# A two-layer encoder trunk in float32 on one NeuronCore: Strassen's algorithm for most of the gated layers' first product

## The reference

```python
D_MODEL, BATCH, SEQ, DEPTH = 1024, 1, 512, 2
FFN_DIM = ((8 * D_MODEL // 3 + 127) // 128) * 128            # 2816

def _conv_glu_ffn(x, w_in, conv_w, conv_b, w_down):
    gate, up = jnp.split(x @ w_in, 2, axis=-1)
    gate = lax.conv_general_dilated(gate, conv_w[:, None, :], window_strides=(1,),
        padding=[(1, 1)], dimension_numbers=('NWC', 'WIO', 'NWC'),
        feature_group_count=FFN_DIM) + conv_b
    return (jax.nn.gelu(gate, approximate=False) * up) @ w_down

def reference(x, ...):
    for i in range(DEPTH):
        if i % 2 == 0: h = _chunked_spatial_gating(x, ...)
        else:          h = _diff_attention(x, positions, ...)
        x = _layer_norm(DEEPNORM_ALPHA * x + h, ln_g[i, 0], ln_b[i, 0])
        h = _conv_glu_ffn(x, f_w_in[i], f_conv_w[i], f_conv_b[i], f_w_down[i])
        x = _layer_norm(DEEPNORM_ALPHA * x + h, ln_g[i, 1], ln_b[i, 1])
    return x
```

## Time and profile before

| | |
|---|---|
| median of three runs | 1276.57 us (1276.24 to 1276.88) |
| the profiled execution, its own time | 1277.31 us |
| its span, first to last instruction | 1275.6 us |
| PE busy | 1266.0 us, 99% |
| DVE, ACT, POOL busy | 650.2, 459.4, 165.1 us |
| mean granted clock of PE | 0.999 of full |

### The profile page before, as it was taken

One profiled execution on the slowest core, in us unless ns is written; L12 is line 12 of the kernel. 1 busy time (PEld: TensorE's weight loads), 2 busy tenths in 40 slices (PEclk: granted clock), 3 DMA queues, 4 the chain that ended last, 5 costly groups with the idle time before them and its releaser, 6 DMA issues.

```text
span 1275.6 us, 15660 instructions
## 1 busy us (share of the span) xinstructions
PE 1266.0 (99%) x6096; PEld 1055.6 (83%) x6096; DVE 650.2 (51%) x890; ACT 459.4 (36%) x553; POOL 165.1 (13%) x159
## 2 busy tenths in 40 slices
PE   9999999999999999999999999999999999999997
PEld 7888888889888888888888877788988888888886
DVE  3637877346343434433372777775743334343346
ACT  3422333322232323322314588775143222232230
POOL 3001100040000000000224444453100000000001
PEclk9999999999999999999999999999999999999999
DMA  8434564250433232222522334235032333232221
GB/s 269 146 96 124 173 176 147 89 185 2 131 99 99 87 99 80 98 97 99 188 74 71 100 105 124 91 108 166 33 99 99 99 99 99 99 99 100 96 102 66
DMA packets 104652, 140.64 MB, mean 110 GB/s; under 512 B 9440, under 2 KB 81464, under 8 KB 104352
## 3 DMA queue, kind: packets, MB, share of 16 engines
q1 hardware_dynamic: 95024, 127.81, 31.2%
q0 software_dynamic: 9440, 12.11, 2.9%
q10 hardware_dynamic: 144, 0.13, 0.0%
HBM read 137.85 MB, written 10.52 MB: 116 GB/s over the span
## 4 chain that ended last, share of the span: by engine, by line
PE 98%; DVE 1%; DMA 0%; ACT 0%; issue 0%; POOL 0%; DVEq 0%; SPq 0%; POOLq 0%
PE bank L1263 31%; PE bank L1267 31%; PE bank L1266 31%; PE bank L1654 1%; PE bank L1508 1%; PE bank L1273 1%; PE bank L1406 1%; DMA w_raw<-in_a_w_in_dram 0%; PE bank L1511 0%; PE bank L1397 0%; DVE prob L1141 0%; DVE w_lo L875 0%; PE bank L1684 0%; PE bank L1683 0%; ACT w_hi L514 0%
## 5 line engine op out<-in xcount | busy, mean ns | idle before, releaser
L1263 PE MATMUL bank<-xt_hi,w_hi 128*128 128x512 f32 (+1 forms) x1008 | 380.8, 378 | 0.0
L1267 PE MATMUL bank<-xt_hi,w_lo 128*128 128x512 f32 (+1 forms) x1008 | 378.8, 376 | 0.0
L1266 PE MATMUL bank<-xt_lo,w_hi 128*128 128x512 f32 (+1 forms) x1008 | 378.7, 376 | 0.0
L765 DVE TENSOR_TENSOR w_lo<-w_raw,w_hi 128x2048 fp32r<-128x2048 f32 x79 | 180.8, 2289 | 184.6 <-ACT w_hi L468 158.3
L1263 PEld LDWEIGHTS bank<-xt_hi,w_hi 128*128 128x128 f32 x1008 | 189.7, 188 | 36.4 <-issue 3.0
L1267 PEld LDWEIGHTS bank<-xt_hi,w_lo 128*128 128x128 f32 x1008 | 189.7, 188 | 34.5
L1266 PEld LDWEIGHTS bank<-xt_lo,w_hi 128*128 128x128 f32 x1008 | 189.8, 188 | 33.9
L468 ACT CAST w_hi<-w_raw 128x2048 fp32r<-128x2048 f32 x53 | 101.3, 1913 | 185.6 <-PE bank L1263 179.6
L1263 PE MATMUL bank<-w_hi,s_hi 128*128 128x512 f32 x416 | 162.1, 390 | 0.0
L1266 PE MATMUL bank<-w_lo,s_hi 128*128 128x512 f32 x416 | 161.9, 389 | 0.0
L1267 PE MATMUL bank<-w_hi,s_lo 128*128 128x512 f32 x416 | 161.8, 389 | 0.0
(11 more groups left out here) (209 smaller groups left out, 1488.3 us busy)
## 6 DMA issues: line engine op xcount, KB each, us to landing
w_raw<-in_f_w_in_dram SPq DMA_DIRECT2D x44, 1024.0 KB, 5.1
w_raw<-in_f_w_down_dram SPq DMA_DIRECT2D x22, 1024.0 KB, 4.8
w_raw<-in_a_w_in_dram SPq DMA_DIRECT2D x14, 1024.0 KB, 6.1
bias_by_query_key<-bias_by_distance POOLq DMA_DIRECT2D x8, 1024.0 KB, 16.0
w_raw<-in_a_w_out_dram SPq DMA_DIRECT2D x8, 1024.0 KB, 7.0
w_raw<-in_b_w_qkv_dram SPq DMA_DIRECT2D x16, 512.0 KB, 4.8
bias_sb<-bias_by_query_key SPq DMA_DIRECT2D x32, 256.0 KB, 2.6
w_raw<-in_b_w_qkv_dram SPq DMA_DIRECT2D x4, 1024.0 KB, 5.4
```

The lines of the kernel that those rows point to most:

```text
L765: dve.tensor_tensor(lo_of(u), w_raw[:, u % 2, :], hi_of(u), ALU.subtract).then_inc(w_lo_done, 1)
L1263: ins = pe.matmul(o, a_hi, b_hi, start=start, stop=False)
L1266: pe.matmul(o, a_hi, b_lo, start=False, stop=False)
L1267: return pe.matmul(o, a_lo, b_hi, start=False, stop=stop)
```

## The change

Pairs 0 and 1 of each gated layer stay as they were. The other nine pairs, 18 units (`NV`), are computed by Strassen's algorithm, in the form with seven products and shared sums. A unit's weights are a matrix of two by two cells: two halves of the 1024 rows (A11 and A12 the upper and the lower rows of block 0, the raw cells (1, 0) and (1, 1) those of block 1), each cell 512 rows x 128 columns, which is 128 partitions x 512 values. The tokens' matrix has two by two quarters of 512 rows x 256 tokens. For each unit POOL forms four sums of cells (S1, S2, S4, S3), ACT casts seven cells, DVE subtracts five for their low parts and POOL two (A12 and A22), and PE runs seven products of 4 k-steps x 3 matmuls with 256 tokens as the moving operand, each into a bank of its own. DVE adds them up, one add of 128 x 256 for each, seven a unit, into `gate_y` (gate units) or `act` (up units); ACT copies the first. The taps read `gate_y` from SBUF instead of a bank, and the product of gate and up reads `conv` and `act`, both in SBUF. The four sums of the tokens' quarters (T1 to T4, `comb`) are made once a layer, during pair 1, by DVE and POOL. The first `U_D` unit's low part is made on POOL instead of DVE.

In the diff, `Fori` bodies keep their counts by `count`, which turns a unit and a step into a semaphore value.

```diff
@@ buffers (shortened) @@
+    w_sum = at("w_sum", 80 * KB, [P, 2, UC])
+    gate_y = at("gate_y", R_U + 76 * KB, [P, 2, S])
+    more_hi = [[at(f"more_hi{c}{k}", MORE_HI[c][k], [P, NB], F32R) for k in range(3)] for c in range(2)]
...
@@ ScalarE @@
+                def split_weights(v, i=None):
+                    u, par, c = u0 + 4 + v, (u0 + v) % 2, v % 2
+                    act_e.wait_ge(w_landed[par], landed_count(u) + (0 if i is None else i * 16))
+                    act_e.wait_ge(w_used, u - 1 + (0 if i is None else i * 2))
+                    for m, k in ((A11, 0), (A12, 1)):
+                        act_e.copy(as_cell(cell_hi(c, par, m)), raw_cell(par, 0, k)).then_inc(cell_hi_done, 1)
+
+                def split_sums(v, i=None):
+                    par, c = (u0 + v) % 2, v % 2
+                    for n, m in enumerate((S1, S2, S4, S3)):
+                        act_e.wait_ge(sum_done, count(l, 4, v, n + 1, i))
+                        act_e.copy(cell_hi(c, par, m), cell_sum(c, par, m)).then_inc(cell_hi_done, 1)
+                    act_e.copy(as_cell(cell_hi(c, par, A22)), raw_cell(par, 1, 1)).then_inc(w_hi_done, 1)
...
@@ VectorE @@
+                def combine():
+                    dve.wait_ge(up_mm, m0 + 2)
+                    step(dve.tensor_tensor(comb[T1][:, :, :], x_cell(xt_hi, 0, 1), x_cell(xt_hi, 0, 0), ALU.subtract), 1)
...
+                def low(v, i, m, n):
+                    par, c = (u0 + v) % 2, v % 2
+                    dve.wait_ge(cell_hi_done, count(l, 6, v, n, i))
+                    hi, lo = cell_hi(c, par, m), cell_lo(c, par, m)
...
+                        ins = dve.tensor_tensor(lo, cell_sum(c, par, m), hi, ALU.subtract)
+                    ins.then_inc(cell_lo_done, 1)
+
+                def add(v, i, to, have, m, n, after=0):
...
+                    dve.wait_ge(cells_mm, count(l, 7, v, m + 1, i))
+                    dve.tensor_tensor(to, have, cell_bank(m), ALU.add).then_inc(cells_read, 1)
+
+                def unit(v, i=None):
...
+                    if v:
+                        last_add(v - 1, i)
+                    if v < NV - 1:
+                        low(v + 1, i, A11, 1)
+                    if v and v % 2 == 0:
+                        gated(v - 1, i)
+                    if v % 2:
+                        left(f, 0, gate_y[:, 0, :])
+                        left(f, 1, gate_y[:, 1, :])
+                    dve.wait_ge(m1_copied, count(l, 1, v, 1, i))
+                    add(v, i, q11, q22, M2, 1)
+                    if v % 2:
+                        right(f, 0, gate_y[:, 0, :])
+                        right(f, 1, gate_y[:, 1, :])
+                    if v < NV - 1:
+                        low(v + 1, i, S1, 3)
+                    add(v, i, q12, q22, M6, 2)
+                    if v < NV - 1:
+                        low(v + 1, i, S2, 4)
+                    add(v, i, q21, q12, M7, 3, 2)
+                    if v < NV - 1:
+                        low(v + 1, i, S4, 5)
+                    add(v, i, q12, q12, M5, 4)
+                    add(v, i, q22, q21, M5, 5, 3)
+                    if v < NV - 1:
+                        low(v + 1, i, S3, 6)
+                    else:
                         stationary(act, S_D[l], 0)
+                    add(v, i, q12, q12, M3, 6, 4)
...
@@ TensorE @@
+                def unit(v, i=None):
+                    multiply(v, i, M1, A11, x_cell(xt_hi, 0, 0), x_cell(xt_lo, 0, 0), 1)
+                    multiply(v, i, M2, A12, x_cell(xt_hi, 1, 0), x_cell(xt_lo, 1, 0))
+                    if v == 0:
+                        pe.wait_ge(comb_lo_done, 4 * l + 4)
+                    multiply(v, i, M6, S2, comb_hi[T2], comb_lo[T2])
+                    multiply(v, i, M7, S3, comb_hi[T3], comb_lo[T3])
...
+                    multiply(v, i, M5, S1, comb_hi[T1], comb_lo[T1])
+                    multiply(v, i, M3, S4, x_cell(xt_hi, 1, 1), x_cell(xt_lo, 1, 1))
...
+                    multiply(v, i, M4, A22, comb_hi[T4], comb_lo[T4])
...
@@ GpSimd @@
+            def sums(l, v, i=None):
...
+                pool.wait_ge(w_landed[par], landed_count(u) + (0 if i is None else i * 16))
+                pool.wait_ge(w_used, u - 1 + (0 if i is None else i * 2))
+                to = {m: as_cell(cell_sum(c, par, m)) for m in (S1, S2, S3, S4)}
+                pool.tensor_tensor(to[S1], raw_cell(par, 1, 0), raw_cell(par, 1, 1), ALU.add).then_inc(sum_done, 1)
...
+                pool.tensor_tensor(to[S2], to[S1], raw_cell(par, 0, 0), ALU.subtract).then_inc(sum_done, 1)
...
+                pool.tensor_tensor(to[S4], raw_cell(par, 0, 1), to[S2], ALU.subtract).then_inc(sum_done, 1)
+                pool.tensor_tensor(to[S3], raw_cell(par, 0, 0), raw_cell(par, 1, 0), ALU.subtract).then_inc(sum_done, 1)
+                pool.wait_ge(cell_hi_done, count(l, 6, v, 2, i))
+                pool.tensor_tensor(as_cell(cell_lo(c, par, A12)), raw_cell(par, 0, 1), as_cell(cell_hi(c, par, A12)),
+                                   ALU.subtract).then_inc(pool_lo_done, 1)
+                pool.wait_ge(w_hi_done, u + 1 + (0 if i is None else i * 2))
+                pool.wait_ge(cell_lo_done, count(l, 5, v, 5, i))
+                pool.tensor_tensor(as_cell(cell_lo(c, par, A22)), raw_cell(par, 1, 1), as_cell(cell_hi(c, par, A22)),
+                                   ALU.subtract).then_inc(w_lo_done, 1)
```

312 lines of the change are left out of this document (244 added, 68 removed).

## The result

| | before | after |
|---|---|---|
| median | 1276.72 us (1276.24 to 1276.89, four runs) | 1360.18 us (1358.27 to 1363.5, four runs) |
| the profiled execution, its own time | 1277.31 us | 1363.5 us |
| its span | 1275.6 us | 1361.4 us |
| PE, DVE, ACT, POOL busy | 1266.0, 650.2, 459.4, 165.1 us | 1276.2, 977.3, 555.0, 556.3 us |
| mean granted clock of PE | 0.999 | 0.972 |

The ratio is 1.065, with a 95% interval of 1.064 to 1.067: the change costs 83.5 us, where 65 were forecast. Nearly all of it lies in the two stretches that the diff touches.

A forecast was written before the change was run, and what follows sets the result against it. PE bounded the old kernel; DVE and POOL's shared path with its chain would bound the new. 18 x (12.3 - 10.88) + 7 - 4 + 4 = 32.6 us a layer, 65 for two, gave 1342 us, range 1288 to 1385.

The forecast's parts named there:

- the exclusion of DVE and POOL: In the Strassen units, DVE operations with two SBUF inputs and POOL's block each other; 0.45 us each, shared path at least 11.1.
- the chain: Per unit, a round of waits: POOL's first five operations, DVE's remaining work, POOL's A22; 12.1 us, 12.3 with hand-offs.
- The unit: Time per Strassen unit in the nine pairs: 12.3 us taken, between 11.1 and 13.0, against 10.88 before.
- six of eight get between: In a unit's round, six of DVE's eight two-SBUF-input operations fall between POOL's first five: 6 x 0.45 = 2.7 us.
- Start: Ahead of each layer's unit 0, PE waits for the tokens' sums and low parts: about 7 us (0 to 9).
- Lead: The first three units of a layer find prepared cells and run nearer to 11 us: -4 us a layer.
- End: After a layer's last unit, the next product waits for the low part of `act`: +4 us (1 to 6).
- Sum: Per layer, 18 x (12.3 - 10.88) + 7 - 4 + 4 = 32.6 us; two layers 65 us.
- Rival D: PE's waits lower the granted clock; one unit at half clock a start gives 1362 us; chance 0.05 for more than 1385.
- The price of a matmul: In PE's products, 120.0 ns per 256-token matmul, read from the rows, so 84 make 10.08 us a unit.
- A: In the units, the shared path doesn't bind or blocking is short, so PE bounds: 28.8 us less, 1248; chance 0.11.
- B: In the units, the shared path binds but is packed almost without rest: 11.1 us a unit, 1285 us; chance 0.08.

The follow-up runs named there:

- The experiments on both sides of the exclusion: Two kernels against the changed one: DVE's eight operations per unit reading a PSUM bank as one input, 1268.8 us; POOL's four weight sums left out, 1267.1 us.
- the experiment on the start: Sums of the tokens' quarters begun earlier, against the changed kernel with `conv` in PSUM and A22's wait shortened (1276.5 us): 1261.7 us.
- the first experiment: Changed kernel with DVE's low parts (units 1 to 17), taps and gated products reading a PSUM bank in place of a second SBUF input: 1268.8 us.

## Why the prediction was right, and where its sizes were off

- **Sign and mechanism.** Forecast 1342, measured 1360.2, 18 more, within what was allowed for. PE's own unit did shrink from 10.88 to 10.1 us (forecast 10.08), each engine's work alone would have fitted in it, and the exclusion of DVE and POOL with the chain made 12.5 of it, as the prediction had it. The experiments on both sides of the exclusion carry this; it was read from few rows of a gauge and of a subtraction. Its length was put two ways there: "exclude each other for their whole length", but priced at 0.45 us for a DVE operation whose own is 0.60 to 0.66. The price held and the wording did not: in the loop POOL starts an operation every 1.7 us beside DVE's, where POOL's 1.25 and DVE's 0.60 to 0.66 one behind the other would be 1.85 to 1.91.
- **The unit.** 12.3 was taken, in the loop the mean of a pair is 12.6. The chain's terms, from the rows above: POOL's first five operations 8.5 us, forecast 6.25 + 2.7 = 8.95; POOL's wait 1.89 and 3.76, 2.8 in the mean, forecast 1.9 plus hand-offs of 0.2; A22 1.25, forecast 1.28. So the term that was too small is what DVE still has to do when POOL stops: in the taps' unit DVE has four taps to get through beside POOL, 6.6 us, and when POOL stops at 499.03 it has the end of low S1, an add, low S2 and another add to do ahead of "low S4, two adds, low S3". That alternation was not foreseen. Over 17 steps the 0.3 us make 5 us a layer. The step "six of eight get between" was too high by one: POOL's five operations took 2.3 us more than their 6.25, five times 0.45.
- **Start.** 7 us forecast, 7.70 measured, and 8.7 with all that came before unit 0 (348.22 against 339.54). The parts were less near: the first block sum on DVE took 3.41 beside POOL in place of the 1.14 forecast, four low parts 8.23, and POOL's operations of 1024 values 2.4 (forecast 2.5), up to 4.32 when blocked (DVE, then POOL, in order of time):

```profile
323.30 3.41 DVE L1181 TENSOR_TENSOR comb<-xt_hi 128x1024 f32<-128x1024 f32 x1
...
338.27 8.23 DVE L1208 TENSOR_TENSOR comb_lo<-comb,comb_hi 128x1024 fp32r<-128x1024 f32 x4
...
318.81 2.42 POOL L2153 TENSOR_TENSOR comb<-xt_hi 128x1024 f32<-128x1024 f32 x1 [18.11 <-PE bank L1474]
321.30 4.32 POOL L2154 TENSOR_TENSOR comb_part<-xt_lo 128x1024 f32<-128x1024 f32 x1
```

- **Lead.** -4 forecast. The first two distances are 11.1 and 12.2, the last 13.3; against 17 x 12.6 that is only -1.2. This term rested on no row, and it was 2.8 us a layer too good.
- **End.** +4 forecast; +3.9 by the first layer's rows (2.96 + 11.86 about the first and last copy, less one unit of 10.88); PE's wait for the low part of `act` is 4.11.
- **Sum.** Start 8.7, seventeen distances 17 x (12.53 - 10.88) = 28.1 and end 3.9 make 40.7 us for the first layer, forecast 7 + 21.6 + 4 = 32.6. The second layer adds 83.0 - 40.7 = 42.3; it holds the 2.9 us at half clock behind the first layer's pairs. The 2.8 us of the span behind the second's are the same once more. So some 5.7 of the 85.8 us are a term that the sum didn't have: the next product's start at half clock.
- **Rival D.** The clock did fall to its lower level at each start, as the rival had it, but its price was overrated and its place only half right. At most 5 us of PE's work ran at half clock there, worth 1.2 us by the experiment on the start. The dearer falls were not named: those behind each layer's last unit, 2.9 and 2.8 us. In the loop such stretches show no cost: PE is not the bound there. One of them (granted clock third from the end),

```profile
388.00:390.00 2.00, 2.00 (x11) 2.00 (x11) 2.00 (x4) 0.69 (x1) 1.55 (x2) 0.50 0.00 0
```

lies in a stretch where the copies stay 12.5 to 12.7 us apart as everywhere. The four executions of this kernel do order by their granted clock, from 1358.3 us at 0.979 to 1363.5 at 0.972; in which stretch they differ isn't known, since only the last was traced.

- **The price of a matmul.** The prediction took 120.0 ns from the rows over the 109 ns that the formula in "TensorE: Matmul & The Clock Gate" in the Trainium skill, section "Back-to-back issue gap", gives for 256 columns. The kernel of the first experiment has 10.14 us a unit, 120.7 ns each, so the rows of before were the better guide. What the prediction left out is that the Trainium skill gives this formula for an isolated matmul, and says that in a stream with weight loads it counts too little at few columns and too much at 512. Here it counts too little at both: at 512 columns the rows have 226.7 ns and the formula 216.
- **Rivals A and B.** A (1248) asked for a path that doesn't bind. The kernel with the inputs moved is that case, and it takes 1268.8, not 1248: the starts' 2 x 7.7 us stay, with their stretch of half clock, and A had left them out; that is most of the 21 us between the two. B (11.1 us a unit) would have needed DVE's low parts ready each time; with the chain loosened it is 11.90, and 11.1 was reached only with three of the eight operations freed.
